# Three orders of work beside the weight stream: the split of a chunk fetched early, the last transposes of the gated activations, and the sums taken out of the accumulators before the last projection

## The reference, cut to what matters

```
# first block, end
u = square(relu(h @ w_up))                     # 2048 -> 8192
x = x + rms_norm(u @ w_down, norm_mlp_post)    # 8192 -> 2048
# second block
u    = rmsnorm(x, norm_w);  proj = u @ w_in    # split into many parts, hg_g the last
y_b  = h_b * silu(hg_g);    y = concat([y_a, y_b])
h    = h + y @ w_out
e    = p @ w_pe
gate = sigmoid(rmsnorm(h, pe_norm_w) @ w_pg)
out  = rmsnorm(h + gate * e, final_norm_w)
```

## Time and profile before

| what | value |
|---|---|
| median of 3 runs | 2007.04 us |
| the profiled execution's own time | 2006.48 us |
| its span, first to last instruction | 2004.6 us |
| TensorE matmuls busy | 1986.4 us, 99% |
| TensorE weight loads busy | 1650.4 us, 82% |
| VectorE busy | 1171.2 us, 58% |
| ScalarE busy | 985.2 us, 49% |
| weights and inputs read | 364.94 MB, 183 GB/s |

### The profile page before, as it was taken

One profiled execution on the slowest core, in us unless ns is written; L12 is line 12 of the kernel. 1 busy time (PEld: TensorE's weight loads), 2 busy tenths in 40 slices (PEclk: granted clock), 3 DMA queues, 4 the chain that ended last, 5 costly groups with the idle time before them and its releaser, 6 DMA issues.

```text
span 2004.6 us, 22298 instructions
## 1 busy us (share of the span) xinstructions
PE 1986.4 (99%) x9216; PEld 1650.4 (82%) x9216; DVE 1171.2 (58%) x1081; ACT 985.2 (49%) x975; POOL 40.3 (2%) x42
## 2 busy tenths in 40 slices
PE   9999999999999999999999999999999999999998
PEld 7888888888888888888888888888898888887786
DVE  5746546645566644443356666677386858675555
ACT  6345544445445444444455555564556445454444
POOL 0000000000000000000000000000000000230000
PEclk9999999999999999999999999999999999999999
DMA  9554555455657366666555555574456444356443
GB/s 322 197 199 146 169 189 179 168 189 190 217 168 264 119 182 183 188 189 186 181 181 197 199 190 189 189 243 162 162 166 210 150 152 164 127 210 206 156 166 108
DMA packets 185437, 368.48 MB, mean 184 GB/s; under 512 B 6776, under 2 KB 14200, under 8 KB 184440
## 3 DMA queue, kind: packets, MB, share of 16 engines
q1 hardware_dynamic: 184472, 366.08, 55.1%
q10 hardware_dynamic: 864, 0.99, 0.1%
HBM read 364.94 MB, written 2.10 MB: 183 GB/s over the span
## 4 chain that ended last, share of the span: by engine, by line
PE 96%; issue 1%; DVE 1%; ACT 1%; DMA 0%; SPq 0%; POOLq 0%; POOL 0%; DVEq 0%
PE acc L1350 90%; PE mis L1350 4%; PE mis L1353 2%; ACT hi L486 1%; DMA raw<-in_w_in 0%; DVE m L860 0%; DVE lo L878 0%; SPq L342 0%; ACT ath L507 0%; DVE atl L908 0%; ACT spare L486 0%; DVE atl L882 0%; DVE xs L860 0%; ACT m L475 0%; DVE atl L915 0%
## 5 line engine op out<-in xcount | busy, mean ns | idle before, releaser
L878 DVE TENSOR_TENSOR lo<-raw,hi 128x2048 fp32r<-128x2048 f32 (+1 forms) x332 | 752.7, 2269 | 645.8 <-ACT hi L486 643.5
L1350 PE MATMUL acc<-hi,ath 128*128 128x512 f32 (+1 forms) x2672 | 1049.7, 393 | 5.7 <-DVE atl L908 1.6
L1350 PE MATMUL acc<-hi,atl 128*128 128x512 f32 (+1 forms) x2672 | 1034.7, 387 | 0.0
L1350 PE MATMUL acc<-lo,ath 128*128 128x512 f32 (+1 forms) x2672 | 1033.4, 387 | 0.0
L486 ACT ACTIVATE hi<-raw 128x2048 fp32r<-128x2048 f32 (+1 forms) x332 | 626.9, 1890 | 386.6 <-PE acc L1350 372.6
L1350 PEld LDWEIGHTS acc<-hi,ath 128*128 128x128 f32 x2672 | 501.9, 188 | 107.4 <-issue 4.2
L1350 PEld LDWEIGHTS acc<-hi,atl 128*128 128x128 f32 x2672 | 501.5, 188 | 102.2
L1350 PEld LDWEIGHTS acc<-lo,ath 128*128 128x128 f32 x2672 | 502.1, 188 | 98.1 <-issue 0.5
L475 ACT ACTIVATE m<-mis 128x512 f32<-128x512 f32 (+1 forms) x95 | 49.7, 523 | 217.0 <-PE mis L1353 188.0
L475 ACT ACTIVATE m<-acc,st 128x512 f32<-128x512 f32 (+2 forms) x104 | 69.8, 671 | 114.9 <-PE acc L1350 114.2
L860 DVE TENSOR_TENSOR m<-m 128x512 f32<-128x512 f32 (+2 forms) x119 | 72.3, 607 | 20.7 <-ACT m L475 15.7
(11 more groups left out here) (117 smaller groups left out, 553.8 us busy)
## 6 DMA issues: line engine op xcount, KB each, us to landing
raw<-in_w_in SPq DMA_DIRECT2D x134, 1024.0 KB, 5.1
raw<-in_w_up SPq DMA_DIRECT2D x64, 1024.0 KB, 5.5
raw<-in_w_down SPq DMA_DIRECT2D x64, 1024.0 KB, 5.0
raw<-in_w_out SPq DMA_DIRECT2D x32, 1024.0 KB, 5.1
raw<-in_w_pg SPq DMA_DIRECT2D x16, 1024.0 KB, 5.1
raw<-in_w_in SPq DMA_DIRECT2D x12, 688.0 KB, 4.2
raw<-in_w_a SPq DMA_DIRECT2D x8, 1024.0 KB, 5.1
raw<-in_w_b SPq DMA_DIRECT2D x8, 1024.0 KB, 5.0
```

Source lines behind the costliest of these rows:

```text
L878: e.tensor_tensor(lo, raw, hi.bitcast(F32), ALU.subtract).then_inc(s_lo.on("lo", n))
L1350: return e.matmul(o, a, b, start=start, stop=stop)
```

## The change

`EARLY` puts the split of chunk 242 at n = 237 instead of 236. 237 is the first chunk of the turnover, which now goes through the list `ahead[n0 - 3]` = [239, 242] on ScalarE and VectorE; so chunk 242 comes behind 239 in both, and in SyncE's fetches too. For n0 = 112 the list is [111], as it was. The last two units of "y" move by half a chunk each, to before `products(310, 0)` and `products(310, 1)`, on TensorE, ScalarE and VectorE. And at n = 323 VectorE does `evac` before `low(325)`.

```diff
-EARLY = {N_UP: (100, 101, 102), N_IN2: (231, 233, 236)}
+EARLY = {N_UP: (100, 101, 102), N_IN2: (231, 233, 237)}
...
-        fill_early("y", N_RES - 4, [(N_RES + 2, 1), (N_RES + 3, 0)])
+        fill_early("y", N_RES - 4, [(N_RES + 2, 0), (N_RES + 2, 1)])
...
 # scalar
             def turnover(name, n0):
                 b = chunks[n0 - 1][2]
-                high(n0 - 1)
+                for c in ahead[n0 - 3]:
+                    high(c)
                 square(b, 0)
...
 # vector
             def turnover(name, n0):
                 b = chunks[n0 - 1][2]
-                low(n0 - 1)
+                for c in ahead[n0 - 3]:
+                    low(c)
                 row_mean(n0 - 1, 0, b)
...
 # vector, main loop
                 last = n == blocks[chunks[n][2]][3][-1]
+                if n == N_PG - 1:
+                    evac(chunks[n][2])
                 for c in ahead.get(n, ()):
                     if c not in spare:
                         low(c)
...
                 if last:
-                    if n < N_ALL - 1:
+                    if n < N_ALL - 1 and n != N_PG - 1:
                         evac(b)
-                    else:
+                    elif n == N_ALL - 1:
                         finish(b)
```

## The result

The changed kernel took 2001.47 us, the median of 10 runs (2000.89 to 2002.6), against 2007.16 us for the kernel before in 10 runs (2006.23 to 2007.53): ratio 0.9973, 95% interval 0.9966 to 0.9981. The forecast was 2002.0 us, with a range from 2001.0 to 2003.6.

A forecast was written before the change was run, and what follows sets the result against it. TensorE was taken as the bound, its matmuls busy for 99% of the span, so only its stalls could be saved. Three stalls, 1.40 + 1.90 + 1.74 = 5.04 us, off the median 2007.04 gave 2002.0 us, range 2001.0 to 2003.6.

The forecast's parts named there:

- The two idle columns: At TensorE's three waits: matmuls' idle column sums to 4.2 us (2002.8), loads' idle notes to 5.82 us (2001.2).
- Rival (d): At TensorE's three waits, only the matmuls' idle column comes back, giving 2002.8 us; chance 0.10, within the main case's 0.78.
- (a): One of TensorE's three waits stays or is replaced, most likely at the turnover: 2003.4 us, otherwise 2003.7 to 2003.9; chance 0.14.
- (b): No gain, because TensorE arrives earlier at a wait timed by the fetches: 2007.0 us; chance 0.05.
- (c): Slower, because VectorE holds `low(312)` behind two units and can idle: 2008.7 us if 9 us later; chance 0.03.
- Each microsecond beyond is lost: At `low(312)`, each microsecond of lateness beyond the 2.3 us margin costs TensorE a microsecond.
- The prediction's other figure: Whole kernel: the profiled execution of the kernel before, 2006.48 us, less the three stalls' 5.04 us, would be 2001.4 us.

The follow-up runs named there:

- edit 1: Only chunk 242 split and fetched behind 239, against the kernel before: run alone, 2005.44 us, ratio 0.9993.
- VectorE's order alone: Changed kernel with "y" placed as before on TensorE and ScalarE; only VectorE takes the second unit ahead of `low(312)`: 2001.57 us.
- the two doses that cost nothing: Changed kernel plus unread VectorE operations: two of 1.2 us ahead of `low(239)`, 2001.85 us; or one of 2.3 us ahead of `low(312)`, 2001.68 us.
- edit 3 alone: Only the sums moved ahead of `low(325)` on VectorE, against the kernel before: 2005.29 us, ratio 0.9992.
- with two doses: Changed kernel plus two unread VectorE operations of 128x2048 (4.5 us) ahead of `low(312)`: 2002.91 us, ratio 0.9981 to the kernel before.

## Why the prediction was right

**The price of each stall.** Measured from start to start, 1.40 + 1.90 + 1.74 = 5.04 us was forecast. The changed kernel's trace shows the same stretches shorter by exactly these three numbers, and the rest of the kernel behind the head shorter by 5.02 us. That these agree to 0.02 us is partly luck, with spans given to 0.1 us. The two idle columns would have said 4.2 and 5.8. Rival (d) falls by 0.8 us in the trace; the medians alone would not decide it.

**Where each gain comes from.** The times worked out for the new order, shifted by what lies ahead of them, came out within 0.1 us in the cases below. `hi` of 239 starts at the end of chunk 236, with a margin of 1.0 us. The second `atl` was worked out for 1815.8; less 1.40 for edit 1 and plus 0.72 for the later head that is 1815.1, and it ended at 1815.06. `low(312)` was to start at 1816.9, that is 1816.2 here, and started at 1816.18. The sums were to start at 1896.2, that is 1893.6, and started at 1893.58. Two margins came out somewhat wider than worked out, that of the first `atl` at 2.8 us instead of 2.5 and that of `low(312)` at 2.5 instead of 2.3, mostly because TensorE came to chunks 311 and 312 0.13 us later.

**No rival had a share.** (a) needed a late `hi` or `lo` of 239. When one was made late by ScalarE's order, 0.9 us came back, as the margin of 1.0 us says. (b) needed a wait timed by transfers, and each edit kept its full gain alone. (c) is a real mechanism that this change does not set off: work added ahead of `low(312)` cost nothing with 2.3 us put in and 1.16 us with 4.6. "Each microsecond beyond is lost" was a little low, since 0.93 us of lateness cost 1.16.

**What was not forecast.** The median came out 0.53 us below the forecast. The medians fell by 5.69 us beside the first before and by 5.4 to 5.45 against the later ones (those across sessions); the three stalls account for 5.02 of it. The start of the first long stretch, which no edit touches, lies anywhere from 111.85 to 113.37 us in the ten traces, and the changed kernel's own runs spread over 1.7 us. The prediction's other figure, 2001.4 us for a run with the head of the trace before, fits: the profiled run of the changed kernel took 2002.1 us, with a head 0.72 us longer. From there on four kernels without any of these stalls (the changed one, VectorE's order alone, and the two doses that cost nothing) agree within 0.12 us, 1887.67 to 1887.79. That the rest of the medians' difference comes from the head is argued from this, not shown: there is only one trace of each kernel. What makes the head vary was not tried. The traces differ there in two things at least. In eight of them the chain that ended last goes through the first transfer of the activations (`m<-in_xt`), which took 6.32 to 7.76 us. And in the trace with the latest stretch (edit 3 alone, 113.37 us) the granted clock was 0.57 on average from 7 to 15 us, with matmuls 0.43 us apart (the lower of TensorE's two levels), after TensorE had waited 1.8 us for a `lo`; in the changed kernel's trace it was 1.00. The transfer alone does not put the ten in order: with two doses it took 7.40 us, and the stretch began at 111.91.

## What to carry to other kernels

When one engine is full, look only at its own waits, and at each ask what stands ahead of the needed instruction in the queue of the engine named, and then in the queue of the engine before that: the list of waits names the last link only. Price a stall from start to start across it, and for every instruction pushed back work out when it is wanted. A gain of 0.07 to 0.1% per edit is below what these medians could tell, but not below what a trace can. Measure such an edit from the start of an undisturbed stretch behind the part that varies and ahead of all that the edit touches, to the end.

## What the runs showed of the hardware

A stall costs more than the idle column of the matmuls shows. Where ScalarE kept its order, `lo` was 0.77 us late (its end at 1374.48, wanted at 1373.71) and the column says 0.67, but the 14 steps across it took 0.97 us more. The first matmul behind a stall is followed after 0.34 us and the next few after 0.23 to 0.24, instead of 0.227.

The start of the first long stretch varies by 1.5 us over the ten traces, one of each kernel, though no edit touches what lies ahead of it. That is about what each of the three edits is worth (1.40, 1.90 and 1.74 us).
